# Expert stage of a two-block network: rows stationary instead of weights, weights split into high and rest, streamed in 8 KB pieces

## The chip, the core and the metric

The kernel runs on one NeuronCore of a Trainium2 chip. Its engines are TensorE (PE, with weight loads shown apart as PEld), VectorE (DVE), ScalarE (ACT), GpSimd (POOL) and SyncE (SP), which here mostly issues DMAs. Data lives in HBM (DRAM), in SBUF (128 partitions) and in PSUM, where TensorE writes. The metric is the device time of one execution in microseconds; less is better.

## What is computed

Two blocks of a network over 1024 tokens of 1024 features, in float32. The change touches the second half of the first block, a mixture of experts: each token picks a group, then two of its eight experts, and each expert is a gated two-layer product. Cut to that part:

```
g_sel = argmax(tok @ w_group + b_group)
top_l, top_i = top_k(e_logits[g_sel], 2)
weight = p_group * softmax(top_l)
expert = g_sel * 8 + top_i                    # 32 experts
# pairs (token, expert) sorted by expert into blocks of rows
xb = tok[rows_tok]
a = xb @ w_gate[e]                            # [rows,1024] @ [1024,512]
u = xb @ w_up[e]                              # [rows,1024] @ [1024,512]
y = (silu(a) * u) @ w_down[e]                 # [rows,512] @ [512,1024]
out = zeros.at[row_tok].add(y * weight)
```

## The kernel before

`build_program` runs `first_mixer`, `mixture` and `second_block` one after another. `mixture` has four stages, each a block of five engine programs that synchronise by semaphores: `norm_to_T` (normalises the rows, stores them in DRAM as `normed_rows`, turns them for the router and lets TensorE compute the logits), `route` (picks experts, gives each pair a row in a block), `experts`, and `combine`, which gathers each token's two result rows from the DRAM tensor `expert_rows`.

A block of `experts` holds up to CAP = 88 rows of one expert; there are 32 blocks, one for each expert, and a branch for overfull experts, which is not taken in these runs. For each block:

- POOL copies the block's 88 row numbers to `block_ids` (L1405) and gathers the rows from DRAM into one of three slots of `rows` by an indirect DMA (L1408).
- PE turns them with eight transposes into `x_ps` (`turn`, L1426), and DVE copies them to `xT` (`x_out`, L1512).
- PE computes gate and up, 64 matmuls each (L1436): a 128x128 piece of the weights is the stationary operand and 88 columns of `xT` stream. The operands are plain float32.
- ACT takes the silu (L1485), DVE multiplies by up into `hidT` (L1519).
- PE computes down, 16 matmuls (L1449): 88 columns of `hidT` stationary, 512 columns of `w_down` streaming.
- ACT and DVE copy the halves of `y_ps` into the single buffer `y_rows` (L1491, L1525), and SP stores them (L1378).

Weights come in three slots of 6 MB each (gate, up and down of an expert, 2 MB each), issued by SP (L1106) as soon as the matmuls that read a slot are done. Gate and up rows are 2 KB in DRAM, down rows 4 KB. The order on PE is gate and up of block b, turn of block b+1, down of block b. The engines' programs are `Fori` loops over blocks. The first two slots are loaded during `norm_to_T`, the third during `route`.

Elsewhere in the kernel large products are made of three float32r matmuls (`product`, L107): each operand is split into a high part, rounded to float32r by ACT (L147), and a rest, made by DVE (L151) as the difference; high by high, high by rest and rest by high are summed in PSUM.

Of the kernel before, what the change touches and what calls it, by code (L numbers as in the profile page):

```python
# [53 lines left out]
WSLOTS = 3  # L54
# [377 lines left out]
def norm_to_T(nc, m, name, hT, gamma=None, gamma_row=None, rows_out=None, x_ready=None, res_out=None,  # L432
# [13 lines left out]
    with ExitStack() as mem:  # L446
# [75 lines left out]
        def _(dve):  # L522
# [9 lines left out]
            for t in range(TT):  # L532
# [10 lines left out]
                else:  # L543
                    if t == 0:
                        dve.wait_ge(g_in, 16)
                    if t >= 2:
                        dve.wait_ge(turned, t - 1)
                        dve.wait_ge(stored[t % 2], 16 * (t // 2))
                    nc.vector.scalar_tensor_tensor(out=scaled[:, t % 2, :], in0=m.res[:, t, :],
                                                   scalar=rstd[:, t:t + 1], in1=g_row[:], op0=ALU.mult,  # L550
# [496 lines left out]
class Router:  # L1047


    def __init__(self, nc, m, mem):  # L1050
        def sb(name, shape, dt=F32):
            return mem.enter_context(nc.sbuf_tensor(name, shape, dt))

        self.w = sb("router_w", [P, KT, NL])
        self.b = sb("router_b", [P, NL])
        self.before = sb("before", [P, P])
        self.idx = sb("index_row", [P, 2, EXPERTS])
        self.limits = sb("limits", [P, FULL_BLOCKS - 1])
# [4 lines left out]
        self.ps = mem.enter_context(nc.psum_tensor("route_ps", [P, 2, BANK], F32))  # L1063

    def load(self, sp, A):
        sp.dma_start(self.w[:], A["w_router"].rearrange("(k p) n -> p k n", p=P)).then_inc(self.loaded, 16)
# [17 lines left out]
class ExpertWeights:  # L1084
# [3 lines left out]
    def __init__(self, m):  # L1088
        self.gate, self.up, self.down = [], [], []
        self.gate_in = [m.sem(f"w_gate_in{s}") for s in range(WSLOTS)]  # L1090
        self.up_in = [m.sem(f"w_up_in{s}") for s in range(WSLOTS)]
        self.down_in = [m.sem(f"w_down_in{s}") for s in range(WSLOTS)]

    def add_place(self, nc, mem):
        s = len(self.gate)
        self.gate.append(mem.enter_context(nc.sbuf_tensor(f"w_gate_sb{s}", [P, KT, D_EXPERT], F32)))
        self.up.append(mem.enter_context(nc.sbuf_tensor(f"w_up_sb{s}", [P, KT, D_EXPERT], F32)))
        self.down.append(mem.enter_context(nc.sbuf_tensor(f"w_down_sb{s}", [P, D_EXPERT // P, D], F32)))

    def load(self, engine, A, s, e, used=None):  # L1100

        for i, (w, name, arrived) in enumerate(((self.gate, "w_gate", self.gate_in), (self.up, "w_up", self.up_in),
                                                (self.down, "w_down", self.down_in))):
            if used is not None:
                engine.wait_ge(*used[i])
            engine.dma_start(w[s][:], A[name][0, bass.ds(e, 1)].rearrange("o (k p) n -> p (o k) n", p=P)) \  # L1106
                .then_inc(arrived[s], 16)


def route(nc, m, A, router, weights):  # L1110
# [3 lines left out]
    with ExitStack() as mem:  # L1114
# [50 lines left out]

        @block.sync
        def _(sp):

            weights.load(sp, A, WSLOTS - 1, WSLOTS - 1)
# [148 lines left out]
def experts(nc, m, A, weights):  # L1318


    with ExitStack() as mem:
# [4 lines left out]
        S = WSLOTS  # L1326
        FE = D_EXPERT // P
        idx = sb("block_ids", [CAP, S], I32)
        rows = sb("rows", [CAP, S, D])
        xT = sb("xT", [P, KT, CAP])  # L1330
        act_out = sb("gate_act", [P, FE, CAP])
        hidT = sb("hidT", [P, FE, CAP])
        y = sb("y_rows", [CAP, D])
        ps_x = mem.enter_context(nc.psum_tensor("x_ps", [P, KT, P], F32))
        ps_h = mem.enter_context(nc.psum_tensor("h_ps", [P, 2, FE, P], F32))
        ps_y = mem.enter_context(nc.psum_tensor("y_ps", [P, 2, BANK], F32))

        idx_set = [sem(f"block_ids_set{s}") for s in range(S)]
        rows_in = [sem(f"rows_in{s}") for s in range(S)]

        turned = sem("rows_turned")
        xT_done = sem("xT_done")
        gate_mm = sem("gate_mm")
        up_mm = sem("up_mm")
        act_done = sem("gate_act_done")
        hid_done = sem("hid_done")
        down_mm = sem("down_mm")
        y_left = sem("y_left")
        y_right = sem("y_right")
        y_out = sem("y_stored")  # L1350
        block = mem.enter_context(nc.Block())

        waited_sp = sem("waited_sp")
        waited_pool = sem("waited_pool")
        ROUNDS, REST = EXPERTS // S, EXPERTS % S
        LAST = EXPERTS - 1

        OVER_SLOT = REST
# [11 lines left out]
        def _(sp):  # L1370
            def reload(s, e, read):

                weights.load(sp, A, s, e, used=((gate_mm, read), (up_mm, read), (down_mm, read)))

            def store(b):
                sp.wait_ge(y_left, b + 1)
                sp.wait_ge(y_right, b + 1)
                sp.dma_start(m.y_dram[bass.ds(b * CAP, CAP), :], y[:]).then_inc(y_out, 16)  # L1378

            with sp.Fori(0, ROUNDS - 1) as i:  # L1380
                for s in range(S):
                    reload(s, i * S + (S + s), i * S + (s + 1))
                    store(i * S + s)
            for b in range(EXPERTS - S - REST, EXPERTS):
                if b + S < EXPERTS:
                    reload(b % S, b + S, b + 1)
                store(b)

            def over(j):
                e = sp.value_load(m.over_table[0:1, bass.ds(j, 1)], min_val=0, max_val=EXPERTS - 1)  # L1390
                reload(OVER_SLOT, e, j + EXPERTS)
                store(j + EXPERTS)

            count = over_blocks(sp, over)

            sp.wait_ge(y_out, (count + EXPERTS) * 16)
            sp.sem_inc(waited_sp, 1)

        @block.gpsimd
        def _(pool):  # L1400
            def gather(s, b, use, read=None):

                if read is not None:
                    pool.wait_ge(turned, read)
                nc.gpsimd.tensor_copy(idx[:, s:s + 1], m.row_ids[:, bass.ds(b, 1)]).then_inc(idx_set[s], 1)  # L1405
                pool.wait_ge(idx_set[s], use + 1)
                pool.sem_inc(waited_pool, 1)
                pool.indirect_dma_start(rows[:, s, :], None, m.hn_dram,  # L1408
                                        bass.IndirectOffsetOnAxis(ap=idx[:, s:s + 1], axis=0)).then_inc(rows_in[s], 16)

            for s in range(S):
                gather(s, s, 0)
            with pool.Fori(1, ROUNDS) as i:
                for s in range(S):
                    gather(s, i * S + s, i, read=(i - 1) * S + (s + 1))
            for s in range(REST):
                gather(s, ROUNDS * S + s, ROUNDS, read=(ROUNDS - 1) * S + s + 1)
            over_blocks(pool, lambda j: gather(OVER_SLOT, j + EXPERTS, j + ROUNDS, read=j + EXPERTS))

        @block.tensor  # L1420
        def _(pe):
            def turn(s, use):

                pe.wait_ge(rows_in[s], (use + 1) * 16)
                for k in range(KT):
                    last = nc.tensor.transpose(ps_x[:, k, 0:CAP], rows[:, s, k * P:(k + 1) * P], m.ident[0:CAP, 0:CAP])  # L1426
                last.then_inc(turned, 1)

            def gate_up(s, use, b):
                pe.wait_ge(xT_done, b + 1)  # L1430
                for i, (w, arrived, done) in enumerate(((weights.gate, weights.gate_in, gate_mm),
                                                        (weights.up, weights.up_in, up_mm))):
                    pe.wait_ge(arrived[s], (use + 1) * 16)
                    for f in range(FE):
                        for k in range(KT):
# [1176 lines left out]
```

## Time and profile before

| | us |
|---|---|
| median of 3 runs | 3107.51 |
| lowest and highest | 3106.19, 3111.67 |
| span of the profiled execution | 3109.3 |
| mean TensorE clock granted, share of full | 0.943 |

The profile is of one execution. No time of its own is given for it beside the span, from the first to the last instruction, which is 1.8 us above the median of the runs. Busy time of an engine is the time in which an instruction of it ran. Matmuls are pipelined: one that shows as 390 ns long may start 227 ns after the one before it, so the pace is read from starts, or from a count in a window.

### The profile page before, as it was taken

How to read it: one execution, taken by the hardware profiler on the slowest of the kernel's cores; microseconds unless marked ns; L12 is line 12 of the kernel's file. 1: busy time of each engine (PE TensorE's matmuls, PEld its weight loads, DVE VectorE, ACT ScalarE, POOL GpSimd, SP SyncE). 2: the span in 40 equal slices, each digit the busy share in tenths (PEclk: the TensorE clock that was granted, in tenths of full speed). 3: DMA queues.
4: the chain of work that ended last, by engine and by line, in shares of the span. 5: the costliest groups of instructions: out<-in, count | busy, mean ns of one | idle time of the engine just before them, and what ended most of it. 6: DMA issues, size and time to landing. Idle time of an engine off the chain costs nothing. (4 is left out here: it accounts for less than half of the span.)

```text
span 3109.3 us, 32228 instructions
## 1 busy us (share of the span) xinstructions
PE 2834.6 (91%) x13544; PEld 2152.5 (69%) x13544; DVE 948.2 (30%) x1118; ACT 597.1 (19%) x833; POOL 196.0 (6%) x176
## 2 busy tenths in 40 slices
PE   6799998785999999999299998999898999998998
PEld 2388553575878787878177776666576888886877
DVE  5423152423010101010621265111244344433343
ACT  1311111120000000000411254111223222222232
POOL 3210101000000000000420000000002000000000
PEclk9899999785899999999699999999898999999999
DMA  3151322026899999993521001111302111113323
GB/s 117 44 161 40 116 59 81 18 70 257 276 318 320 318 320 316 322 316 117 211 69 47 34 1 47 42 41 34 115 35 74 47 47 47 50 51 122 98 86 108
DMA packets 231333, 388.13 MB, mean 125 GB/s; under 512 B 11422, under 2 KB 110750, under 8 KB 231256
## 3 DMA queue, kind: packets, MB, share of 16 engines
q1 hardware_dynamic: 221768, 358.83, 34.6%
q0 software_dynamic: 9488, 28.22, 2.9%
q8 instruction: 55, 0.90, 0.1%
q14 instruction: 22, 0.18, 0.0%
HBM read 350.41 MB, written 39.74 MB: 125 GB/s over the span
## 5 line engine op out<-in xcount | busy, mean ns | idle before, releaser
L111 PE MATMUL up_ps<-hT_high,w_up_high 128*128 128x512 f32 x704 | 274.7, 390 | 7.3 <-PEq L446 7.3
L112 PE MATMUL up_ps<-hT_rest,w_up_high 128*128 128x512 f32 x704 | 274.6, 390 | 0.0
L113 PE MATMUL up_ps<-hT_high,w_up_rest 128*128 128x512 f32 x704 | 274.5, 390 | 0.0
L1436 PEld LDWEIGHTS h_ps<-xT,w_gate_sb 128*128 128x128 f32 x2048 | 240.1, 196 | 17.1 <-issue 15.9
L1436 PE MATMUL h_ps<-xT,w_up_sb 128*128 128x88 f32 x2048 | 240.5, 280 | 0.0
L1436 PE MATMUL h_ps<-xT,w_gate_sb 128*128 128x88 f32 x2048 | 239.5, 279 | 1.0 <-DVE xT L1512 1.0
L1436 PEld LDWEIGHTS h_ps<-xT,w_up_sb 128*128 128x128 f32 x2048 | 237.8, 196 | 0.0
L1449 PE MATMUL y_ps<-w_down_sb,hidT 128*88 128x512 f32 x512 | 228.7, 600 | 2.6 <-DVE hidT L1519 2.5
L1449 PEld LDWEIGHTS y_ps<-w_down_sb,hidT 128*88 128x88 f32 x512 | 78.4, 158 | 130.8 <-issue 126.5
L111 PE MATMUL down_ps<-w_down_high,prod_high 128*128 128x512 f32 x352 | 139.3, 396 | 20.6 <-DVE w_down_rest L151 12.9
L111 PEld LDWEIGHTS up_ps<-hT_high,w_up_high 128*128 128x128 f32 x704 | 132.6, 188 | 35.2 <-issue 7.7
L1519 DVE TENSOR_TENSOR hidT<-gate_act,h_ps 128x352 f32<-128x352 f32 x32 | 16.7, 521 | 445.6 <-PE h_ps L1436 445.6
L113 PEld LDWEIGHTS up_ps<-hT_high,w_up_rest 128*128 128x128 f32 x704 | 132.6, 188 | 27.8
L112 PEld LDWEIGHTS up_ps<-hT_rest,w_up_high 128*128 128x128 f32 x704 | 132.6, 188 | 27.5
L112 PE MATMUL down_ps<-w_down_rest,prod_high 128*128 128x512 f32 x352 | 138.4, 393 | 0.0
L113 PE MATMUL down_ps<-w_down_high,prod_rest 128*128 128x512 f32 x352 | 138.3, 393 | 0.0
L151 DVE TENSOR_TENSOR w_up_rest<-res,w_up_high 128x1024 fp32r<-128x1024 f32 x44 | 57.0, 1298 | 247.6 <-ACT w_up_high L147 247.6
L111 PE MATMUL gates_ps<-hT_high,gates_w_high 128*128 128x512 f32 x256 | 103.3, 404 | 7.5 <-DVE gates_w_rest L151 7.5
L1491 ACT ACTIVATE y_rows<-y_ps 88x512 f32<-88x512 f32 x32 | 19.0, 593 | 473.4 <-PE y_ps L1449 473.4
L111 PE MATMUL proj_ps<-hT_high,proj_w_high 128*128 128x512 f32 x256 | 100.7, 393 | 7.3 <-PEq L446 7.3
L147 ACT ACTIVATE w_up_high<-res 128x1024 fp32r<-128x1024 f32 x44 | 46.5, 1060 | 295.8 <-PE up_ps L113 295.8
L112 PE MATMUL proj_ps<-hT_rest,proj_w_high 128*128 128x512 f32 x256 | 100.5, 393 | 0.0
(311 smaller groups left out, 4498.7 us busy)
## 6 DMA issues: line engine op xcount, KB each, us to landing
w_gate_sb<-in_w_gate_dram SPq DMA_DIRECT2D x32, 2048.0 KB, 10.2
w_up_sb<-in_w_up_dram SPq DMA_DIRECT2D x32, 2048.0 KB, 11.5
w_down_sb<-in_w_down_dram SPq DMA_DIRECT2D x32, 2048.0 KB, 9.6
res<-in_w_in_dram SPq DMA_DIRECT2D x48, 512.0 KB, 4.0
res<-in_w_up_dram SPq DMA_DIRECT2D x44, 512.0 KB, 3.8
w_down_raw<-in_w_down_dram SPq DMA_DIRECT2D x44, 512.0 KB, 3.6
expert_rows<-y_rows SPq DMA_DIRECT2D x32, 352.0 KB
res<-in_x_dram SPq DMA_DIRECT2D x16, 512.0 KB, 7.2
```

The lines of the kernel that those rows point to most:

```text
L111: nc.tensor.matmul(out, w_high, x_high, start=start, stop=False)
L112: nc.tensor.matmul(out, w_high, x_rest, start=False, stop=False)
L113: return nc.tensor.matmul(out, w_rest, x_high, start=False, stop=stop)
L147: self.nc.scalar.activation(self.high_part[:, s], self.raw[s], ACT.Copy).then_inc(self.high_done[s], 1)
L151: self.nc.vector.tensor_tensor(self.rest_part[:, s], self.raw[s], self.high_part[:, s].bitcast(F32), ALU.subtract) \
L1436: last = nc.tensor.matmul(ps_h[:, i, f, 0:CAP], w[s][:, k, f * P:(f + 1) * P], xT[:, k, :], start=(k == 0), stop=(k == KT - 1))
L1449: last = nc.tensor.matmul(ps_y[0:CAP, half, :], hidT[:, f, :], weights.down[s][:, f, half * BANK:(half + 1) * BANK], start=(f == 0), stop= ...
L1491: nc.scalar.activation(y[:, 0:BANK], ps_y[0:CAP, 0, :], ACT.Copy).then_inc(y_left, 1)
L1519: nc.vector.tensor_tensor(hidT[:], act_out[:], ps_h[:, 1, :, 0:CAP], ALU.mult).then_inc(hid_done, 1)
```

## The change

In `experts` the gathered rows become the stationary operand of gate and up too, and all three products are made of float32r parts. Per block: the turned rows are split by ACT and DVE into `x_high` and `x_rest`; the gate and up weights stream, 512 columns at a time, into one PSUM bank each with 88 rows; silu and the multiplication work on rows; the hidden rows are turned back by four transposes (`turn_hidden`) and split into `hid_high` and `hid_rest`; down is made of parts as well. `in_products` and `out_products` issue 12 matmuls for a unit.

The weights come as units of 1 MB (8 KB on each of the 128 partitions, contiguous in DRAM): two each for gate, up and down. They pass through a ring of seven raw pieces and a ring of five split pieces (`ExpertWeights.high` on ACT, `ExpertWeights.rest` on DVE). `_units` fixes their order: the four gate and up units of expert e, then the two down units of expert e-1. Seven units are loaded during `norm_to_T`, none in `route`.

A partition now holds features 8p to 8p+7 instead of p, 128+p, ...; `norm_to_T` writes its rows in that order (through strided access patterns of one DVE instruction), and the router's weights are loaded to match. The loops are written out. Stores of `y_rows` (now two buffers) move from SP to POOL, and the copy of the row numbers goes away.

The core of the diff:

```diff
-WSLOTS = 3
+UNIT = 2 * D
+RAW_SLOTS = 7
+SPLIT_SLOTS = 5
...
+    def load(self, engine, n):
+        if n >= RAW_SLOTS:
+            engine.wait_ge(self.rest_done, n - RAW_SLOTS + 1)
+        e, i = UNITS[n]
+        engine.dma_start(self.raw[:, n % RAW_SLOTS, :], self.source(e, i)).then_inc(self.raw_in[n % RAW_SLOTS], 16)
+
+    def high(self, act, n):
+        act.wait_ge(self.raw_in[n % RAW_SLOTS], 16 * (n // RAW_SLOTS + 1))
+        if n >= SPLIT_SLOTS:
+            act.wait_ge(self.used, n - SPLIT_SLOTS + 1)
+        self.nc.scalar.activation(self.high_part[:, n % SPLIT_SLOTS, :], self.raw[:, n % RAW_SLOTS, :], ACT.Copy) \
+            .then_inc(self.high_done, 1)
+
+    def rest(self, dve, n):
+        dve.wait_ge(self.high_done, n + 1)
...
-                    for f in range(FE):
-                        for k in range(KT):
-                            last = nc.tensor.matmul(ps_h[:, i, f, 0:CAP], w[s][:, k, f * P:(f + 1) * P],
-                                                    xT[:, k, :], start=(k == 0), stop=(k == KT - 1))
...
+        def in_products(pe, out, s, i):
+
+            for kk in range(KT // 2):
+                k = (i % 2) * (KT // 2) + kk
+                last = product(nc, out[0:CAP, :], (x_high[:, k, :], x_rest[:, k, :]), weights.parts(s, kk * D_EXPERT),
+                               start=(k == 0), stop=(k == KT - 1))
+            return last
...
+            def gather(b):
+                if b >= S:
+                    pool.wait_ge(x_turned, b - S + 1)
+                pool.indirect_dma_start(rows[:, b % S, :], None, m.hn_dram,
+                                        bass.IndirectOffsetOnAxis(ap=m.row_ids[:, b:b + 1], axis=0)) \
+                    .then_inc(rows_in[b % S], 16)
+
+            def store(b):
+                pool.wait_ge(y_left, b + 1)
+                pool.wait_ge(y_right, b + 1)
+                pool.dma_start(m.y_dram[b * CAP:(b + 1) * CAP, :], y[:, b % S, :]).then_inc(y_out[b % S], 16)
+
+            gather(0)
+            gather(1)
+            for b in range(EXPERTS):
+                if b + S < EXPERTS:
+                    gather(b + S)
+                store(b)
...
+            turn(0)
+            for b in range(EXPERTS):
+                gate_up(b)
+                if b + 1 < EXPERTS:
+                    turn(b + 1)
+                if b:
+                    down(b - 1)
+                turn_hid(b)
+            down(EXPERTS - 1)
...
+            for b in range(EXPERTS + 1):
+                if b:
+                    hid_in(b - 1)
+                if b >= 2:
+                    y_half(b - 2)
+                if b < EXPERTS:
+                    for i in range(4):
+                        ahead(in_at(b, i))
+                    hidden(b)
+                    if b + 1 < EXPERTS:
+                        x_in(b + 1)
+                if b:
+                    ahead(out_at(b - 1, 0))
+                    ahead(out_at(b - 1, 1))
```

(S is 2 in the new `experts`; `ahead(n)` splits unit n+4; the last loop shown is DVE's.)

On POOL, in the middle of the expert stage, before the change: each gather stands behind a small copy and behind nothing else.

```order
L1405 COPY block_ids<-row_ids 88x1
L1408 DMA rows<-normed_rows,block_ids 88x1024
L1405 COPY block_ids<-row_ids 88x1
L1408 DMA rows<-normed_rows,block_ids 88x1024
L1413 UNCONDITIONAL_BRANCH
```

At the same place after the change (the store on L1497 was on SP before):

```order
L1490 DMA rows<-normed_rows,row_ids 88x1024 x3
L1497 DMA expert_rows<-y_rows 88x1024
L1490 DMA rows<-normed_rows,row_ids 88x1024
L1497 DMA expert_rows<-y_rows 88x1024
L1490 DMA rows<-normed_rows,row_ids 88x1024
L1497 DMA expert_rows<-y_rows 88x1024
```

The gather of block b+3 now comes behind the store of block b, so it waits for what the store waits for.

On DVE, one block of the loop before:

```order
L1519 TENSOR_TENSOR hidT<-gate_act,h_ps 128x352
L1508 REGISTER_ALU
L1512 COPY xT<-x_ps 128x704
L1524 REGISTER_ALU
L1525 COPY y_rows<-y_ps 88x512
```

And DVE's rows for one block after the change, from one split of the turned rows to the next:

```order
L1445 TENSOR_TENSOR x_rest<-x_ps,x_high 128x704
L1153 TENSOR_TENSOR expert_rest<-expert_raw,expert_high 128x2048 x2
L1452 TENSOR_TENSOR hid_rest<-hid_ps,hid_high 128x352
L1459 COPY y_rows<-y_ps 88x512
L1153 TENSOR_TENSOR expert_rest<-expert_raw,expert_high 128x2048 x4
L1437 TENSOR_TENSOR expert_hid<-gate_act,expert_up_ps 88x128x4
L1445 TENSOR_TENSOR x_rest<-x_ps,x_high 128x704
```

Three instructions a block have become ten, six of them over 2048 elements, and the copy of `y_rows` stands behind `hid_rest`.

## Rows read from the trace of the kernel before

**Rows 1.** The page: the span, and TensorE's busy time over it.

```profile
span 3109.3 us, 32228 instructions
PE 2834.6 (91%) x13544; PEld 2152.5 (69%) x13544; DVE 948.2 (30%) x1118; ACT 597.1 (19%) x833; POOL 196.0 (6%) x176
```

**Rows 2.** Busy time by stretch: columns in the first line; the expert stage.

```profile
core 0: us, PE busy (x) PEld busy (x) DVE busy (x) ACT busy (x) POOL busy (x), PEclk, DMA share, GB/s
763.00:785.00 22.00, 22.00 (x103) 22.00 (x104) 0.00 (x0) 0.46 (x1) 0.98 (x1) 0.50 0.37 121
...
791.00:1483.00 692.00, 689.38 (x4726) 544.54 (x4724) 65.21 (x94) 32.77 (x62) 32.53 (x56) 1.00 0.86 292
```

**Rows 3.** Timeline of one block: start us, us, engine, line.

```profile
1005.53 7.31 PE L1436 MATMUL h_ps<-xT,w_up_sb 128*128 128x88 f32 x64
...
1012.67 0.77 PE L1426 MATMUL x_ps<-ident,rows 88*128 88x88 f32 x8
...
1013.64 7.07 PE L1449 MATMUL y_ps<-w_down_sb,hidT 128*88 128x512 f32 x16 [0.19 <-DVE hidT L1519]
...
1020.55 7.27 PE L1436 MATMUL h_ps<-xT,w_gate_sb 128*128 128x88 f32 x64
...
1027.66 7.31 PE L1436 MATMUL h_ps<-xT,w_up_sb 128*128 128x88 f32 x64
```

**Rows 4.** Busy time by stretch: steady float32r products of 128x512 (feed-forward).

```profile
2400.00:2800.00 400.00, 400.00 (x1767) 331.20 (x1766) 163.29 (x130) 99.92 (x93) 0.00 (x0) 1.00 0.17 49
```

**Rows 5.** Groups of instructions (xcount | busy us, mean ns | idle before): work on DVE and ACT.

```profile
L151 DVE TENSOR_TENSOR w_down_rest<-w_down_raw,w_down_high 128x1024 fp32r<-128x1024 f32 x44 | 53.9, 1225 | 17.0 <-ACT w_down_high L147 17.0
L1292 DVE TENSOR_TENSOR at_row<-r_of,count_row 128x1408 f32<-128x1408 f32 x1 | 1.6, 1626 | 0.0
L1512 DVE COPY xT<-x_ps 128x704 f32<-128x704 f32 x32 | 28.5, 892 | 11.0 <-PE x_ps L1426 8.4
L1519 DVE TENSOR_TENSOR hidT<-gate_act,h_ps 128x352 f32<-128x352 f32 x32 | 16.7, 521 | 445.6 <-PE h_ps L1436 445.6
L1525 DVE COPY y_rows<-y_ps 88x512 f32<-88x512 f32 x32 | 22.0, 687 | 205.7 <-PE y_ps L1449 205.7
L147 ACT ACTIVATE w_down_high<-w_down_raw 128x1024 fp32r<-128x1024 f32 x44 | 46.0, 1044 | 6.0 <-DMA w_down_raw<-in_w_down_dram 6.0
L1491 ACT ACTIVATE y_rows<-y_ps 88x512 f32<-88x512 f32 x32 | 19.0, 593 | 473.4 <-PE y_ps L1449 473.4
```

**Rows 6.** Busy time by stretch: DMA with many loads queued, and in one block.

```profile
710.00:720.00 10.00, 10.00 (x49) 10.00 (x48) 0.00 (x0) 0.00 (x0) 0.00 (x0) 0.50 1.03 396
...
1005.53:1027.66 22.13, 21.94 (x155) 17.47 (x154) 2.10 (x3) 1.06 (x2) 1.16 (x2) 1.00 0.95 316
```

**Rows 7.** The gathers: issue (ns min/median/max) and landing, 1000 to 1400 us; the first one's timeline.

```profile
L1408 POOL DMA_INDIRECT rows<-normed_rows,block_ids x18: 980/984/987, 1014.7 to 1389.0; - x18
...
DMA to landing us min/median/max: 8.1/8.9/10.7
...
755.73 1.08 POOL L1408 DMA_INDIRECT rows<-normed_rows,block_ids  x1 [0.98 <-POOL block_ids L1405]
...
760.54 1.43 PE L1426 MATMUL x_ps<-ident,rows 88*128 88x88 f32 x8 [6.51 <-DMA rows<-normed_rows,block_ids]
```

**Rows 8.** Timeline of `combine`: gathers alone and beside DVE.

```profile
1494.37 0.94 POOL L1578 DMA_INDIRECT y_pairs<-expert_rows,pair_row  x1 [0.30 <-issue]
...
1498.10 2.60 DVE L1607 SCALAR_TENSOR_TENSOR res<-y_pairs,pair_w,res 128x1024 f32<-128x1024 f32 x2 [0.65 <-DMA y_pairs<-expert_rows,pair_row]
...
1498.56 1.63 POOL L1578 DMA_INDIRECT y_pairs<-expert_rows,pair_row  x1 [0.30 <-issue]
```

**Rows 9.** Stores issued by POOL (ns min/median/max), and the end of the stage.

```profile
L640 POOL DMA_DIRECT2D expert_rows<-res x23: 513/513/786, 156.5 to 167.9; - x23
...
1483.09 0.69 DVE L1525 COPY y_rows<-y_ps 88x512 f32<-88x512 f32 x1 [7.19 <-PE y_ps L1449]
...
1488.11 0.97 POOL L1578 DMA_INDIRECT y_pairs<-expert_rows,pair_row  x1 [98.11 <-SPq L1548]
```

**Rows 10.** Busy time by stretch: granted clock as float32r products of 512 columns begin.

```profile
2358.00:2362.00 4.00, 4.00 (x17) 3.24 (x17) 0.00 (x0) 0.00 (x0) 0.00 (x0) 0.94 0.54 148
```

More of the change, by code:

```diff
@@ L1100, in load, with __init__ @@
[L1100 to L1107, printed above, removed]
+    def __init__(self, nc, m, mem, A):
+        self.nc = nc
+        self.raw = mem.enter_context(nc.sbuf_tensor("expert_raw", [P, RAW_SLOTS, UNIT], F32))
+        self.raw_in = [m.sem(f"expert_raw_in{s}") for s in range(RAW_SLOTS)]
+        self.high_done = m.sem("expert_high_done")
+        self.rest_done = m.sem("expert_rest_done")
+        self.used = m.sem("expert_unit_used")
+        self.gate = A["w_gate"][0].rearrange("e (p k) n -> e p (k n)", p=P)
+        self.up = A["w_up"][0].rearrange("e (p k) n -> e p (k n)", p=P)
+        self.down = A["w_down"][0].rearrange("e (p f) n -> e p (f n)", p=P)
@@ new lines, in in_products, with out_products @@
+        def in_products(pe, out, s, i):
[4 more added lines that the diff above has]
+            return last
+        def out_products(pe, s, i):
+            for ff in range(FE // 2):
+                f = i * (FE // 2) + ff
+                for half in range(2):
+                    last = product(nc, ps_y[0:CAP, half, :], (hid_high[:, f, :], hid_rest[:, f, :]),
+                                   weights.parts(s, ff * D + half * BANK), start=(f == 0), stop=(f == FE - 1))
+            return last
@@ L1370, in _ @@
         def _(sp):
[L1371 to L1383, printed above, removed]
@@ L1396, in _ @@
-            sp.wait_ge(y_out, (count + EXPERTS) * 16)
-            sp.sem_inc(waited_sp, 1)
+                sp.wait_ge(weights.rest_done, j * 6 + N_UNITS)
+                for i in range(6):
+                    w = (weights.gate, weights.up, weights.down)[i // 2]
+                    sp.dma_start(weights.raw[:, i, :], w[bass.ds(e, 1), :, (i % 2) * UNIT:(i % 2 + 1) * UNIT]
+                                 .rearrange("o p n -> p (o n)")).then_inc(weights.raw_in[i], 16)
+            over_blocks(sp, over)
@@ L1420, in _ @@
+            count = over_blocks(pool, over)
+            pool.wait_ge(y_out[0], (count + EXPERTS // S) * 16)
+            pool.sem_inc(waited_pool, 1)
         @block.tensor
         def _(pe):
-            def turn(s, use):
-                pe.wait_ge(rows_in[s], (use + 1) * 16)
-                for k in range(KT):
[L1426 to L1433, printed above, removed]
-                    for f in range(FE):
-                        for k in range(KT):
-                            last = nc.tensor.matmul(ps_h[:, i, f, 0:CAP], w[s][:, k, f * P:(f + 1) * P],
-                                                    xT[:, k, :], start=(k == 0), stop=(k == KT - 1))
-                    last.then_inc(done, 1)
@@ new lines, in hid_in, with y_half, ahead @@
+            def hid_in(b):
+                dve.wait_ge(hid_high_done, b + 1)
+                hid_rest_part(dve)
+            def y_half(b):
+                dve.wait_ge(weights.used, out_at(b, 1) + 1)
+                if b >= S:
+                    dve.wait_ge(y_out[b % S], 16 * (b // S))
+                right(dve, b % S)
+            def ahead(n):
+                if n + SPLIT_SLOTS - 1 < len(UNITS):
+                    weights.rest(dve, n + SPLIT_SLOTS - 1)
+            x_in(0)
+            for n in range(SPLIT_SLOTS - 1):
+                weights.rest(dve, n)
```

370 lines of the change are left out of this document (228 added, 142 removed).

## The prediction

> **What bounds the kernel now.** I read the page first: TensorE is busy 91% of 3109.3 us [rows 1]. The change touches one stage, so next come the stretches of that stage. From 791 to 1483 us TensorE is busy 689.4 of 692 us at full clock, while DVE is busy 65 us and ACT 33 us; the first 22 us ran at half clock [rows 2]. Then the timeline of one block: one start of the up products to the next, 1005.53 to 1027.66, is 22.1 us, made of up (7.0 us to the turn), turn (1.0), down (6.9) and gate (7.1) with no gap over 0.5 us [rows 3]. So TensorE is the bound of this stage, and its neighbour is close: in the same block the DMA engines are busy 95% of the time [rows 6]. The stage lasts from the first gather at 755.7 to the first gather of `combine` at 1488.1, 732.4 us [rows 7, 9]. Everything below is a new time per block, P, and what is added once.
>
> **TensorE.** Removed: 128 matmuls of 88 columns and 16 of 512, 7.0 + 7.1 + 6.9 = 21.0 us. Added: 72 float32r matmuls of 512 columns. Their pace is 400 us / 1767 = 0.226 us [rows 4], where 128 columns are stationary; here it is 88, which can only make the weight load shorter. 72 x 0.226 = 16.3 us. The turn stays (0.8), four transposes come (half of it, 0.4). TensorE needs **17.5 us** a block, 4.5 less than now, if nobody keeps it waiting.
>
> **DVE and ACT.** Six rests of 2048 elements: 1024 take 1.225 and 1408 take 1.626 us [rows 5], a slope of 1.04 us per 1000, so 2048 take 2.29; doubling the first gives 2.45 as the upper bound. That is 13.7 to 14.7. The splits of the turned rows and of the hidden rows, the multiplication and the copy of y are 0.89, 0.52, 0.69, 0.69 (same sizes [rows 5]). The multiplication writes with a stride, which no row shows; between nothing extra and a doubling I take nothing, since it costs 0.7 at most. Sum **16.5 to 17.5 us**, plus ten handovers of some 0.06. ACT: six of 1.93 to 2.09 (from 1.044 [rows 5]) and four small ones under 0.8, about 14 us; it is not the bound. DVE went from 3 instructions to 10 and is now as full as TensorE.
>
> **DMA.** A block moves 6.29 MB of weights, and 0.36 MB each gathered and stored: 7.0 MB. With many loads queued the engines moved 396 GB/s; in the steady block only 316 at a share of 0.95, 333 if always busy [rows 6]. Bounds: 17.7 us and 21.0 us a block. I take a value near the first, 18.2, because seven units may be outstanding, which is the state of the fast row, where one or two loads were outstanding in the slow one; the pieces are also larger, whose effect no row shows. Against this stands a rule of the Trainium skill (DMA: Bandwidth & Descriptors, "Where 436 GB/s comes from"): what one core gets from HBM is about 358 GB/s. Here 396 GB/s were measured from HBM, so this trace does not agree; by the rule a block could not be under 7.0 / 358 = 19.6 us.
>
> **The circle through POOL.** This is the wait that the change adds, and I take it to decide. The gather of block b+3 stands behind the store of block b, which waits for y of block b; ACT and DVE copy that y only behind the split of hidden b+1, which waits for the turn of hidden b+1, the last thing TensorE does before gate and up of b+2. Then TensorE wants the rows of b+3 when gate and up are done. So from one arrival of rows to the next: turn 0.77 [rows 3], down 24 x 0.226 = 5.4 [rows 4], turn of hidden 0.45, hidden high about 0.5, hidden rest 0.52, y copy 0.69 [rows 5], store issue 0.51 [rows 9] and 0.3 between issues [rows 8], handovers 0.3: 9.4 us. Add what DVE is doing when hidden high is ready. After the arrival ACT splits the turned rows (turn and x high: 1.65 us), then highs one unit, so DVE starts its rests at 3.7 and ends the second at 8.3, while hidden high is ready at 7.2: 1.1 us more. Sum 10.5 us. Add the gather from issue to landing: 8.1 to 10.7 us, median 8.9, in the busy stage, 4.8 when the DMA engines were idle [rows 7]. With the median P = **19.4 us**; with 4.8 it is 15.3, and the circle is hidden behind the other bounds; with 10.7 it is 21.2. I take 8.8, close to the median, for two effects that pull apart: the store just ahead in the same queue lengthens the landing, and a P above the DMA bound of 18.2 leaves the load queue short, which shortens it. P = **19.3**.
>
> POOL's issue itself can be held up. A gather took 0.94 us alone and 1.63 beside a DVE instruction with both inputs in SBUF, which began 0.46 us before it and lasts 1.3: it ended with the rest of that instruction added [rows 8]. DVE's rests are such instructions, 2.29 long, and start right after the y copy. Bounds: 0 to 2.3 us a block, of which I put nothing into the sum since the second rest must first get its high part, and keep the end for the range. The Trainium skill states the same as a rule (SBUF — State Buffer, "Who interferes with whom"): a `tensor_tensor` with both inputs in SBUF contends with GpSimd's reads, and the later one blocks fully. By that rule P would be up to 21.6 us, and DVE would in turn wait behind POOL.
>
> **What is added once.** The gather can start at once, 1.2 us earlier than 755.7. Landing 4.8, turn 1.43 at half clock [rows 7], x high 0.8, one high 1.9, one rest 2.3: TensorE's first product is at 765.9. At half clock a unit is 5.4 instead of 2.7; the clock is up 4 to 8 us after such products begin [rows 10], where now it stayed at half over the first 30 us [rows 2]. I add 2.5. At the end: hidden split not covered 1.3, y copy and the wait for the store, now 5.0 from the copy's start at 1483.09 to 1488.11 [rows 9], on POOL some 0.9 more: 5.9. End of the stage = 765.9 + 2.5 + 32 P + 1.3 + 5.9 = **775.6 + 32 P**. It is 1488.1 now, so it breaks even at P = 22.3.
>
> The other edits I cost at nothing: fewer bytes fetched ahead (the seven units are there long before 760, and the third expert's load was on no path), the strided write in `norm_to_T` (ACT's squares and TensorE's logits cover it; uncovered, a microsecond for the first tile), the copy of row numbers (POOL waits anyway). Overfull experts do not occur. The programs are written out, so each engine fetches more instructions through the same DMA engines; no row of this stage prices it.
>
> **Sum.** P = 19.3 gives 775.6 + 617.6 = 1393.2, 94.9 us less than 1488.1. On the span of 3109.3 that is 3014.4; the median of the runs is 1.8 below the span, so **3013 us**.
>
> **Rivals.**
> - *No wait binds.* The gather lands in under 8 us, because the load queue is short when it is issued; TensorE, DVE and DMA all end between 17.5 and 18.5. P = 18.0: 775.6 + 576 = 1351.6, a gain of 136, 2971 us. For it: the circle is self-limiting. Against: three engines within 1 us of each other seldom overlap fully.
> - *DMA is the bound at its steady rate.* If stores and gathers between the loads, not a short queue, made the 333 GB/s, P = 21.0 at worst and 20.6 likely, with nothing else in the way: 775.6 + 659 = 1434.8, 3054 us. The page's 358 GB/s quoted above would be this rival with P = 19.6, 3022 us.
> - *Slower.* The circle with landing at 10.7 us and POOL held up by rests at 2.3 us: 10.5 + 10.7 + 2.3 = 23.5, 775.6 + 752 = 1527.6, a loss of 39.5, 3147 us. It decides from P = 22.3, which means landing plus hold-up of 11.8 us against 8.8 in my sum. For it: rows 8, and 8 KB pieces of load interleaved with the rows. Against: with P over 20 the load queue runs empty.
>
> **Chances.** Forecast (P 18.5 to 20.2) 0.42; no wait 0.22; DMA bound 0.16; a circle of 21 to 22.2, still a little faster or the same, 0.10; slower 0.10. The measurement can tell 0.2%, 6 us, from no change. Faster 0.86, same 0.04, slower 0.10. Range: the low end is P = 17.7 (DMA at 396 GB/s), a gain of 146: 2962. The high end is P = 21.5: 1463.6, a gain of 24: 3083. This leaves out about 0.15.
>
> **What would show it.** Right: blocks 19 to 20 us apart; before most turns TensorE waits 1 to 3 us for the DMA of `rows`; the wait is gone if the gather stands ahead of the store; DVE busy about 85%, DMA share near 0.9 with over 350 GB/s. DMA rival: TensorE's waits are on rests, DVE's on highs, ACT's on the raw pieces' DMA. Wrong altogether: float32r matmuls with 88 stationary columns slower than 0.23 us, rests over 2.5 us, a granted clock that drops in the waits, or gaps put down to issue.

## The result: 1.55% slower, and the profile after

The changed kernel takes 3156.7 us (median; 3155.1 to 3166.3) against 3108.7: a ratio of 1.0155, 95% interval 1.0143 to 1.0167. The forecast was 3013. The span of the profiled execution is 3164.5 us, 55 more than before [rows 1]. Rows of a profile are of one execution and can lie off the medians given: the one of the changed kernel is the slowest of its four, those of e8 (3143.0 us) and e12 (3069.3) are the fastest of theirs, and that of e2 (3157.9) ran slow after the expert stage, at a granted clock of 0.62 from 1600 to 2000 us against 0.98 in the stretch of the expert stage read below, so that e2's time is the median of its other four executions.

```profile
span 3164.5 us, 28100 instructions
...
PE 2753.3 (87%) x11368; PEld 2004.0 (63%) x11368; DVE 1414.1 (45%) x1342; ACT 994.7 (31%) x1089; POOL 244.5 (8%) x176
```

TensorE has less to do (2753 us busy, 2835 before) and the kernel is still longer. Where the time went is read from the gathers: start, duration, line. The first of the stage, two in its middle (the 5th and the 29th), and the first of `combine`:

```profile
755.14 1.09 POOL L1490 DMA_INDIRECT rows<-normed_rows,row_ids  x1 [211.11 <-issue]
...
1538.71 1.02 POOL L1757 DMA_INDIRECT y_pairs<-expert_rows,pair_row  x1 [10.21 <-SPq L1727]
```

The stage lasts 783.6 us instead of 732.4 [rows 7, 9], so 51 of the 55 us are in it. The 5th gather is issued at 831.06 and the 29th at 1404.68: 24 blocks in 573.6 us, **23.9 us a block**. The stretch from 850 to 1350 us:

```profile
core 0: us, PE busy (x) PEld busy (x) DVE busy (x) ACT busy (x) POOL busy (x), PEclk, DMA share, GB/s
850.00:1350.00 500.00, 411.20 (x1754) 274.69 (x1753) 345.48 (x210) 280.81 (x209) 59.10 (x42) 0.89 0.86 294
```

The longest waits from 850 to 1450 us (us in total, times, longest):

```profile
POOL expert_rows L1497 <- DVE y_rows L1459: 521.9, 25, 23.1
ACT x_high L1442 <- PE x_ps L1407: 157.3, 25, 7.7
PEld x_ps L1407 <- DMA rows<-normed_rows,row_ids: 118.3, 25, 5.9
PE x_ps L1407 <- DMA rows<-normed_rows,row_ids: 106.7, 25, 5.5
```

No engine is full: TensorE 82%, DVE 69%, ACT 56%, DMA 0.86 (before, TensorE was busy 689.4 of 692 us [rows 2]). In front of every turn TensorE waits some 4.3 us for the gathered rows, and the clock granted is 0.89 where it was 1.00. The gathers themselves, 1000 to 1400 us, take 2.2 us to issue and 11.4 to land (counted from the start of the issue), where it was 0.98 and 8.9 [rows 7]:

```profile
L1490 POOL DMA_INDIRECT rows<-normed_rows,row_ids x17: 2214/2227/2242, 997.9 to 1380.2; - x17
...
DMA to landing us min/median/max: 10.8/11.4/12.7
```

One turn of the circle through POOL, from the timeline (start, us, engine, line; in brackets the idle time before and what ended it):

```profile
1009.64 1.43 PE L1407 MATMUL x_ps<-ident,rows 88*128 88x88 f32 x8 [4.31 <-DMA rows<-normed_rows,row_ids]
...
1013.70 2.29 DVE L1153 TENSOR_TENSOR expert_rest<-expert_raw,expert_high 128x2048 fp32r<-128x2048 f32 x1 [0.91 <-ACT expert_high L1147]
1015.51 1.92 ACT L1147 ACTIVATE expert_high<-expert_raw 128x2048 fp32r<-128x2048 f32 x1 [1.85 <-PE y_ps L140]
1017.46 2.29 DVE L1153 TENSOR_TENSOR expert_rest<-expert_raw,expert_high 128x2048 fp32r<-128x2048 f32 x1 [1.48 <-ACT expert_high L1147]
1018.04 0.47 PE L1412 MATMUL hid_ps<-ident,expert_hid 88*128 88x88 f32 x4
...
1019.67 0.52 DVE L1452 TENSOR_TENSOR hid_rest<-hid_ps,hid_high 128x352 fp32r<-128x352 f32 x1
...
1020.11 0.68 DVE L1459 COPY y_rows<-y_ps 88x512 f32<-88x512 f32 x1
1021.32 4.49 DVE L1153 TENSOR_TENSOR expert_rest<-expert_raw,expert_high 128x2048 fp32r<-128x2048 f32 x2 [0.54 <-ACT expert_high L1147]
1021.35 0.59 POOL L1497 DMA_DIRECT2D expert_rows<-y_rows  x1 [21.18 <-DVE y_rows L1459]
...
1022.25 2.22 POOL L1490 DMA_INDIRECT rows<-normed_rows,row_ids  x1 [0.30 <-issue]
```

From the arrival of rows (1009.6) to the issue of the next gather (1022.25) are 12.6 us, and 11.4 later, at 1033.68, the next turn begins. Over the 20 rounds from 850 to 1350 us the means are 12.3 and 11.6, together 23.9, the pace that was measured. The clock over the same wait, the turn and the down products:

```profile
1005.40:1009.64 4.24, 0.00 (x1) 0.01 (x1) 2.42 (x2) 0.00 (x0) 0.00 (x0) 0.75 1.00 307
1009.64:1011.10 1.46, 1.46 (x9) 1.46 (x10) 0.00 (x0) 0.00 (x0) 0.00 (x0) 0.50 1.01 421
1011.10:1018.04 6.94, 6.94 (x25) 4.38 (x25) 3.76 (x3) 4.47 (x3) 0.00 (x0) 0.76 0.67 241
```

It falls to half while TensorE waits, the turn runs at half clock, and the stretch of the down products takes 6.9 us, where 24 at the full-clock pace of this trace (0.232 us each) would take 5.6. Not every turn is like this one: 12 of the 20 took 1.43 or 1.44 us, the others 0.8 to 1.1.

### The profile page after: what moved, and what is told of

It reads as the page before. It is cut to its first block and busy times, and to the rows that moved or that the text cites. A ratio compares the mean times of both kernels' runs of the same rounds, so it can differ in the third digit from the quotient of the medians.

```text
span 3164.5 us, 28100 instructions
## 1 busy us (share of the span) xinstructions
PE 2753.3 (87%) x11368; PEld 2004.0 (63%) x11368; DVE 1414.1 (45%) x1342; ACT 994.7 (31%) x1089; POOL 244.5 (8%) x176
## 5 line engine op out<-in xcount | busy, mean ns | idle before, releaser
L1153 DVE TENSOR_TENSOR expert_rest<-expert_raw,expert_high 128x2048 fp32r<-128x2048 f32 x192 | 436.8, 2291 | 112.1 <-ACT expert_high L1147 110.5
L1147 ACT ACTIVATE expert_high<-expert_raw 128x2048 fp32r<-128x2048 f32 x192 | 366.7, 1912 | 71.1 <-PE y_ps L140 53.2
L1407 PE MATMUL x_ps<-ident,rows 88*128 88x88 f32 x256 | 38.9, 320 | 132.0 <-DMA rows<-normed_rows,row_ids 132.0
L138 PE MATMUL y_ps<-expert_high,hid_high 128*88 128x512 f32 x256 | 123.5, 483 | 1.9 <-DVE y_rows L1459 1.9
L1407 PEld LDWEIGHTS x_ps<-ident,rows 88*128 88x128 f32 x256 | 31.7, 193 | 146.0 <-DMA rows<-normed_rows,row_ids 145.6
L139 PE MATMUL y_ps<-expert_rest,hid_high 128*88 128x512 f32 x256 | 119.7, 468 | 0.0
L140 PE MATMUL y_ps<-expert_high,hid_rest 128*88 128x512 f32 x256 | 117.5, 459 | 0.0
L138 PE MATMUL expert_gate_ps<-expert_high,x_high 128*88 128x512 f32 x256 | 103.5, 404 | 5.3 <-DVE expert_rest L1153 5.1
L139 PE MATMUL expert_gate_ps<-expert_rest,x_high 128*88 128x512 f32 x256 | 101.8, 398 | 0.0
```

The source lines that it names most:

```text
L138: nc.tensor.matmul(out, w_high, x_high, start=start, stop=False)
L139: nc.tensor.matmul(out, w_high, x_rest, start=False, stop=False)
L140: return nc.tensor.matmul(out, w_rest, x_high, start=False, stop=stop)
L1147: self.nc.scalar.activation(self.high_part[:, n % SPLIT_SLOTS, :], self.raw[:, n % RAW_SLOTS, :], ACT.Copy) \
L1153: self.nc.vector.tensor_tensor(self.rest_part[:, s, :], self.raw[:, n % RAW_SLOTS, :], self.high_part[:, s, :].bitcast(F32), ALU.subtract) ...
```

## The experiments

The theory: POOL's order closes a circle (rows arrive, down and turn of hidden, copy of y, store, gather, landing), and the circle sets the pace: each gather waits for work that waited for the gather before it. Rivals: the DMA engines are the bound at the rate they show (294 GB/s); or the order is harmless and the landing alone is long, for the size of the pieces or the store's bytes in the same queue. Below, the time of "a block" is taken from the 5th gather to the 29th, as above.

### e1: gathers ahead of stores

```diff
-            gather(0)
-            gather(1)
+            for b in range(S + 1):
+                gather(b)
             for b in range(EXPERTS):
-                if b + S < EXPERTS:
-                    gather(b + S)
+                if b + S + 1 < EXPERTS:
+                    gather(b + S + 1)
                 store(b)
```

> One edit to the changed kernel: POOL issues three gathers at the start and then the gather of block b+3 ahead of the store of block b, so a gather waits only for the turn that frees its slot. If the circle through POOL sets the pace (23.65 us a block in the profile after), TensorE's waits for rows go, blocks come 17.7 to 20 us apart, and the kernel gains 115 to 190 us: 2965 to 3040 us. If instead the DMA engines are the bound at the rate they had in the profile after (293 GB/s), the blocks stay 23 us or more apart, TensorE's waits move to the rests of the weights, and the time stays near 3157 us.

2995.1 us, ratio to the kernel before 0.9627 (0.9611 to 0.9643): 162 us less than the changed kernel, from the order of two instructions. 18.5 us a block. 850 to 1350 us, the gathers, and what ACT waits for:

```profile
850.00:1350.00 500.00, 484.51 (x2262) 326.38 (x2261) 437.76 (x271) 361.08 (x269) 102.18 (x52) 0.99 1.00 371
```

```profile
L1490 POOL DMA_INDIRECT rows<-normed_rows,row_ids x25: 975/2216/8200, 857.8 to 1301.8; - x25
...
DMA to landing us min/median/max: 11.4/12.6/17.4
```

```profile
ACT expert_high L1147 <- DMA expert_raw<-in_w_up_dram: 48.0, 46, 2.8
ACT expert_high L1147 <- DMA expert_raw<-in_w_down_dram: 33.0, 29, 3.0
```

The landing is longer than in the changed kernel (12.6 against 11.4), and TensorE no longer waits for it. The DMA engines are now busy all the time, ACT waits for raw pieces, and the rate is 371 GB/s: 294 was no bound but what the circle asked for. The rival on DMA falls for the changed kernel; once the circle is open it comes next, with TensorE (484.5 of 500 us busy) right beside it.

### e5 and e6: idle POOL is given work

```diff
                 pool.dma_start(m.y_dram[b * CAP:(b + 1) * CAP, :], y[:, b % S, :]).then_inc(y_out[b % S], 16)
+                for i in range(3):
+                    nc.gpsimd.memset(spare[:], 0.0).then_inc(spared, 1)
+                    pool.wait_ge(spared, 3 * b + i + 1)
```

> The changed kernel with three dependent fills of an unused tile on POOL between the store and the gather behind it, some 0.6 us each, 1.8 us a block. POOL is busy 11% of the stage, so by its load it could take them for nothing. If the circle through POOL's order sets the pace, they are added to every block: 29 or 30 blocks x 1.8 = 50 us, at most 58: 3200 to 3215 us. If the circle is not the cause, the time stays at 3157.

3262.5 us, 106 more, twice what was expected; 27.5 us a block, 3.6 more for fills that put off the gather by 1.7 (the store's start to the gather's start 2.6 us instead of 0.9). The rest is in the gather: issue 2.7, landing 13.1.

```profile
L1492 POOL DMA_INDIRECT rows<-normed_rows,row_ids x18: 2397/2722/2745, 858.7 to 1325.6; - x18
...
DMA to landing us min/median/max: 12.4/13.1/14.1
```

> The same three fills in the kernel that gathers ahead of the store. There the circle is open and the DMA engines were busy all the time (share 1.00 at 371 GB/s), so the fills should cost nothing: 2990 to 3000 us. If the pace of that kernel were still set through POOL, it would rise by 50 us as well.

2997.6 us (2995.4 to 3002.2), the same as e1. The same work in the same idle engine costs 106 us in one order and 2.5, less than the spread of the runs, in the other. That is the circle.

### e2 and e12: the store beside and in the queue

```diff
 (POOL)
                 pool.wait_ge(y_left, b + 1)
                 pool.wait_ge(y_right, b + 1)
-                pool.dma_start(m.y_dram[b * CAP:(b + 1) * CAP, :], y[:, b % S, :]).then_inc(y_out[b % S], 16)
 (ACT, y_half)
                 left(act, b % S)
+                act.wait_ge(y_left, b + 1)
+                act.wait_ge(y_right, b + 1)
+                act.dma_start(m.y_dram[b * CAP:(b + 1) * CAP, :], y[:, b % S, :]).then_inc(y_out[b % S], 16)
```

> The order of the changed kernel is kept (POOL still waits for both halves of y of block b before it gathers block b+3), but the store itself is issued by ACT, so it is neither in POOL's program nor in its DMA queue; ACT now waits for DVE's half of y, 1 to 2 us a block. If the wait in the order is the cause, little changes: 0.9 us of issue goes from the circle and perhaps 1 us of landing, 23.65 to some 22 us a block, a gain of 30 to 60 us, and TensorE still waits for rows. If the store's data ahead of the gather in the same queue is the cause, landing falls from 11.4 to 8 us or less and the gain is over 100 us.

3020.7 us, ratio 0.9724 (0.9702 to 0.9745): 136 us less, where I had expected 30 to 60 from the order alone, and over 100 only with a landing of 8 us or less. 19.5 us a block, issue 0.98, landing 8.5:

```profile
L1490 POOL DMA_INDIRECT rows<-normed_rows,row_ids x26: 976/976/979, 860.3 to 1348.7; - x26
...
DMA to landing us min/median/max: 7.2/8.5/11.6
```

TensorE still waits for rows (34.7 us from 850 to 1350, against 88.8 in the changed kernel), so the circle is still there, but it is near the pace of the DMA engines (share 0.97). The edit changes three things: the store leaves POOL's queue, its issue leaves the circle, and ACT's wait for DVE's half puts off the next high, so that no DVE rest runs when the gather is issued. e12 takes out the bytes alone (the rows that it does not write are filled with zeros early in the kernel, so its output is not that of the model):

```diff
-                pool.dma_start(m.y_dram[b * CAP:(b + 1) * CAP, :], y[:, b % S, :]).then_inc(y_out[b % S], 16)
+                pool.dma_start(m.y_dram[b * CAP:b * CAP + 1, :], y[0:1, b % S, :]).then_inc(y_out[b % S], 16)
```

> The changed kernel with its order, but each store from the expert stage writes one row of 4 KB instead of 88 (the other rows are filled with zeros during the first mixer's projection, 32 more stores of zeros there), so the output lacks most of what the experts add. The issue of the store, the order and the wait stay; only its 0.36 MB ahead of the gather in POOL's DMA queue is gone. If these bytes lengthen the landing, it falls from 11.4 to about 9.5 us and blocks come 2 to 4 us closer: 3040 to 3100 us. If the landing is long for the 8 KB pieces and DVE's hold alone, it stays at 11 and the time within 10 us of 3157.

3084.6 us (3069.3 to 3091.7), 72 less; issue 2.27, landing 9.6, clock 0.97, 20.8 us a block:

```profile
L1490 POOL DMA_INDIRECT rows<-normed_rows,row_ids x24: 2076/2268/2299, 863.7 to 1345.1; - x24
...
DMA to landing us min/median/max: 8.8/9.6/12.0
```

```profile
850.00:1350.00 500.00, 439.36 (x2011) 294.12 (x2010) 393.71 (x241) 321.66 (x241) 67.48 (x48) 0.97 0.91 319
```

So 1.8 us of the landing go with the 0.36 MB of the store ahead of the gather in the same queue. In this execution a block becomes shorter by 3.1: the wait shrinks, and with it the time at half clock (arrival to issue is 10.9 us in the mean, 12.3 in the changed kernel). By the medians it is 72 us over 32 blocks, 2.3 each.

### e3: small rows, and e4: the clock

```diff
-        self.gate = A["w_gate"][0].rearrange("e (p k) n -> e p (k n)", p=P)
+        self.gate = A["w_gate"][0].rearrange("e (k p) n -> e p k n", p=P)
```

(up and down alike, and the loads' access patterns to match; the experts then multiply features with other rows of the weights)

> Only the source of the weight loads changes: the units of 1 MB are read as rows of 2 KB (gate, up) and 4 KB (down), as the kernel before did, while the gathered rows keep their new order of features; so the experts multiply features with other rows of the weights, the amount of work and of bytes being the same. If pieces of 8 KB between the gathered rows lengthen the landing, it falls from 11.4 towards the 8.9 us of the kernel before, blocks come 21 to 22 us apart and 50 to 80 us are gained. If piece size does not matter, landing stays at 11 and the time within 10 us of 3157.

3118.2 us (3111.7 to 3128.9), 38 less, short of the 50 to 80 that were expected; 22.7 us a block. Landing (850 to 1350 us):

```profile
DMA to landing us min/median/max: 9.7/10.3/11.1
```

The pieces of 8 KB account for 1.1 us of the 11.4, not for the whole 2.5 over the kernel before.

```diff
             def turn(b):
+                if b:
+                    for _ in range(16):
+                        nc.tensor.matmul(ps_idle[0:CAP, :], x_high[:, 0, :],
+                                         x_high[:].rearrange("p k c -> p (k c)")[:, 0:BANK], start=True, stop=True)
                 pe.wait_ge(rows_in[b % S], 16 * (b // S + 1))
```

> Added: 16 float32r matmuls of 512 columns (some 3.7 us, results unused) in front of each turn, where TensorE waits 4.3 us for rows. The circle stays. If the fall of the clock in that wait is part of the price, the turn takes 0.8 instead of 1.4 us and the down products 5.6 instead of 6.9, blocks come 21.7 us apart and the gain is about 60 us. If the clock does not matter, since the circle is set by DMA, ACT, DVE and POOL, the time stays at 3157 or rises a little.

3139.0 us (3132.6 to 3142.2), 18 less instead of 60. The clock stayed up, 850 to 1350 us:

```profile
850.00:1350.00 500.00, 474.35 (x2192) 318.03 (x2191) 362.23 (x220) 296.25 (x220) 61.89 (x44) 0.99 0.89 307
```

A block took 22.9 us. The part from arrival to issue was 10.7 in the mean (10.4 in most rounds), against 12.3 with the falling clock and 10.5 in my sum; from issue to the next turn it was 12.2 against 11.6, with the landing grown from 11.4 to 12.1. So 1.6 us a block were won and 0.6 lost again; why the landing grew I can't say.

### e7: rests in halves

```diff
-        self.nc.vector.tensor_tensor(self.rest_part[:, s, :], self.raw[:, n % RAW_SLOTS, :],
-                                     self.high_part[:, s, :].bitcast(F32), ALU.subtract).then_inc(self.rest_done, 1)
+        for i in range(2):
+            c = slice(i * UNIT // 2, (i + 1) * UNIT // 2)
+            last = self.nc.vector.tensor_tensor(self.rest_part[:, s, c], self.raw[:, n % RAW_SLOTS, c],
+                                                self.high_part[:, s, c].bitcast(F32), ALU.subtract)
+        last.then_inc(self.rest_done, 1)
```

> The changed kernel with each rest of 2048 elements made by two DVE instructions of 1024. In the profile after each gather's issue took 2.22 us instead of 0.98 and ended with the DVE rest that was running. If the hold-up lasts until the running DVE instruction ends, issue takes at most 1.23 + 0.9, and since the first half began some 0.9 us before, it falls to about 1.3: some 0.9 us a block or 25 to 30 us less, from which later ends of the rests (0.16 us each) may take up to 10: 3125 to 3150 us. If the hold-up is no lock but slow handling under load, issue stays at 2.2 us and the time does not fall.

3144.3 us (3135.3 to 3147.8), 12 less, and the issue of the gather fell from 2.22 to 1.08 us:

```profile
L1493 POOL DMA_INDIRECT rows<-normed_rows,row_ids x22: 1014/1082/1127, 853.0 to 1345.0; - x22
...
DMA to landing us min/median/max: 9.5/10.7/11.5
```

The hold-up ends with the DVE instruction in progress, as expected. A block takes 23.5 us, 0.4 less: of the 1.1 us gained in the issue 0.7 arrived in the landing, and the two halves cost DVE 0.07 more a unit.

### e8: y before hidden

On ACT and on DVE `y_half(b - 2)` moves ahead of `hid_in(b - 1)`.

> The changed kernel with the copies of y of block b ahead of the split of hidden b+1 on ACT and on DVE, instead of behind it. y is ready 0.5 us before the hidden is turned; what comes out of the circle is the turn of hidden (0.5), its high (0.5) and its rest (0.5), but DVE is in a rest until 1.0 us later than that, and TensorE gets its hidden part later only where it has slack. Circle theory: 1 to 2 us a block come out, the fall of the clock with them, 30 to 60 us less, 3095 to 3125 us. If another wait sets the pace, nothing changes.

3157.5 us (3143.0 to 3164.1): no gain in the median, against 30 to 60 expected. The timeline shows why:

```profile
1013.31 2.29 DVE L1153 TENSOR_TENSOR expert_rest<-expert_raw,expert_high 128x2048 fp32r<-128x2048 f32 x1 [1.34 <-ACT expert_high L1147]
...
1015.52 0.68 DVE L1459 COPY y_rows<-y_ps 88x512 f32<-88x512 f32 x1
1016.12 0.51 DVE L1452 TENSOR_TENSOR hid_rest<-hid_ps,hid_high 128x352 fp32r<-128x352 f32 x1
1016.77 0.59 POOL L1497 DMA_DIRECT2D expert_rows<-y_rows  x1 [20.32 <-DVE y_rows L1459]
```

In either order DVE is in a rest until then, so the turn of hidden and its high were not on the path; only the 0.5 us of the hidden rest could leave it. The store is issued 0.57 us after the copy ends, as in the changed kernel (0.56), and the gather's landing was 12.1 us instead of 11.4 in the profiled run. There the part from arrival to issue did fall (11.4 us in the mean, 12.3 before the edit), and half of that went into the landing; the spread of the four executions, 21 us, is wider than what is left. My account of which steps lie in the circle was too simple here, though the circle itself was not at stake.

### e9 to e11: what bounds it once the circle is open

> Both edits together: gathers ahead, and stores issued by ACT. With the circle open the store's queue should not matter any more: DMA moves the same bytes at 371 to 377 GB/s, so the time should be that of gathers first alone, 2985 to 3005 us. If the stores in POOL's queue cost DMA time of their own, it falls by over 10 us; if ACT's wait for DVE's half of y matters, it rises.

2995.3 us, ratio 0.9632 (0.9616 to 0.9649): the same as e1, as expected. Landing is 9.4 us here, 12.6 there; it does not matter. But the DMA engines, though busy all the time, hold up nobody here: no engine waits for raw pieces, and what ACT waits for is that TensorE frees a split piece (850 to 1350 us):

```profile
ACT expert_high L1147 <- PE expert_gate_ps L140: 137.4, 27, 5.4
```

TensorE is busy 97.5% of the time at full clock, 18.0 us of a block by my sum at 0.232 us a product, and waits some 0.5 us a block for DVE (the multiplication and the rest of the turned rows): 18.5, the pace. So once the circle is open TensorE and DMA are bounds of nearly the same height. In e1 it is the raw pieces that come last, as shown above.

> Gathers first, with the weights read as rows of 2 KB (gate, up) and 4 KB (down), so the experts multiply features with other rows of the weights; the amount of work is the same. Now the DMA engines are the bound, so the size of pieces shows in the rate: if 8 KB pieces give a better rate than 2 and 4 KB, the stage moves under 370 GB/s and the time rises by 10 to 40 us over 2995; if only the number of loads outstanding made the rate (333 GB/s per full share before, 371 with seven outstanding), the time stays within 6 us of 2995.

3017.2 us, 22 more than e1, from which it differs in the rows alone. 850 to 1300 us in this kernel, in e1, and in e9:

```profile
850.00:1300.00 450.00, 424.27 (x1959) 283.01 (x1958) 373.26 (x232) 308.20 (x231) 97.14 (x46) 0.98 1.04 361
```

```profile
850.00:1300.00 450.00, 437.40 (x2053) 295.24 (x2052) 395.59 (x246) 326.25 (x244) 99.47 (x48) 0.99 1.02 377
```

```profile
850.00:1300.00 450.00, 438.96 (x2045) 291.27 (x2044) 390.92 (x245) 316.71 (x245) 23.44 (x24) 1.00 1.00 380
```

The DMA engines move 361 GB/s in rows of 2 and 4 KB, and 377 to 380 in pieces of 8 KB. Divided by the share, as the 333 of the kernel before was [rows 6], that is 347, and 370 to 380. So the size of the pieces gives 23 GB/s (e10 to e1), more than the 14 between the kernel before and e10. That those 14 come with the loads outstanding is not shown: in e9 a load lands 8.1 us after its issue (median) and one is issued every 3.1 us, so two or three of 1 MB are outstanding, and the rate is the highest of all.

```diff
-RAW_SLOTS = 7
-SPLIT_SLOTS = 5
+RAW_SLOTS = 9
+SPLIT_SLOTS = 4
```

> Gathers first, with nine raw pieces and four split ones instead of seven and five (the same space). Two more units of 1.05 MB are fetched before the stage, when the DMA engines are idle; if the DMA is the bound of the stage at 377 GB/s, 2.1 MB less are 5.6 us: 2988 to 2992 us. If the splits, only three units ahead of TensorE instead of four, become the bound, the time rises above 3000.

2988.8 us (2988.6 to 2991.8), ratio 0.9617 (0.9601 to 0.9634), the best version, on top of e1's order: 6 us less than e1 for 2.1 MB less in the stage, as a DMA bound says. TensorE is busy 99.9% from 850 to 1050 us, while the pieces fetched ahead last, and 96% from 1050 to 1250.

## Why the prediction was wrong

**The step that failed** is the sum of the circle through POOL. I named it as the wait that decides, and gave 10.5 us from arrival to issue and 8.8 to land, 19.3 in all. Measured, from arrival to issue and from issue to the next turn: 12.3 and 11.6, 23.9 in the mean. Of the 4.6 us that are missing in my sum 2.8 lie in the landing and 1.8 before it. The mechanism held (e1, e5, e6); both parts were taken too short:

| term | mine | measured | shown by |
|---|---|---|---|
| store's bytes ahead in the queue, in the landing | offset against a short load queue | 1.8 | e12 |
| POOL held up by a DVE rest, in the landing | 0 (bound 2.3) | 1.2 of issue, 0.7 in the landing | e7 |
| pieces of 8 KB, in the landing | 0, no row | 1.1 | e3 |
| turn at half clock | 0.77 | 1.43 in 12 of 20 turns | timeline after |
| second rest ends after the arrival | 8.3 | 10.1 in the turn shown | timeline after |

The single effects on the landing overlap and don't add up exactly (1.8 + 0.7 + 1.1 on top of the 8.9 of before would be 12.5; 11.4 was measured). The last two rows of the table are one cause that is missing in my sum: a wait of 4.3 us lowers the clock, the turn and the first down unit run at half clock, the second high waits for that unit, DVE's second rest for the high, and the copy of y for the rest. The wait makes itself longer. e4 shows its size: with the clock up, the part from arrival to issue is 10.7, close to the 10.5 that I had worked out for a full clock. I had put a falling clock only among the things that would make the prediction wrong, not into the price of the circle.

**The reasoning behind the wrong choice**: I set two unknowns of the landing against each other and called the median of before "close". But the row came from a queue with no store ahead of the gather and with DVE mostly idle, and these differences to the new place pointed to longer. The one that points the other way, a DMA queue that runs shorter, is there (share 0.86) and did not win. And the hold-up was put at zero, for the second rest had first to get its high part, with the end kept for the range. [rows 8] had shown a gather held up, and the timeline after has the next rest begin at 1021.32, 0.9 us ahead of the gather.

**What held.** The formula 775.6 + 32 P gives 1540.4 for P = 23.9; the stage ended at 1538.7. TensorE's pace: 0.232 us a product of 512 columns from the timeline (forecast 0.226). Rests took 2.29 us, as worked out, and highs 1.91. The multiplication with the strided write took 1.01 instead of 0.69.

**What met the number by luck.** The rival "slower", P = 23.5 and 3147 us, has the right mechanism and comes within 10 us of 3156.7, and its chance of 0.10 and a range that ended at P = 21.5 were too low. But its terms are not those measured: it has 13.0 for landing and hold-up, where landing, hold-up included, was 11.4, and 10.5 from arrival to issue, where it was 12.3; it knows nothing of the clock, and the two errors cancel. Nor does e1 bear the forecast out, though its 2995 us lie only 18 below it: the forecast had the circle as the bound, and in e1 the circle is open. What e1 does bear out is the DMA term, 18.2 us a block in the sum against a pace of 18.5, with TensorE's 18.0 just below.

**The two rules.** The Trainium skill's rule on the shared port (SBUF — State Buffer, "Who interferes with whom") is borne out for POOL: issue of a gather 2.22 us beside rests of 2.29, 1.08 beside rests of half the length (e7), 0.98 where no rest runs (e2). That DVE waits behind POOL in turn, the other half of what I took from it, is not seen: the two rests from 1021.32 took 4.49 us together, beside the gather's issue. The Trainium skill's figure of about 358 GB/s from HBM for one core (DMA: Bandwidth & Descriptors, "Where 436 GB/s comes from") is not what these runs show: 377 to 380 GB/s over 450 us in e1, e9 and e11, some 5% of it stores.

## What to carry to other kernels

When an instruction is moved to another engine's queue, write down what now stands behind it there, and follow that back to the instruction itself: if it comes round, the sum of the whole round is a bound on the pace, whatever the load of the engines, and giving an idle engine a little work (e5, with e6 beside it) tells at once whether there is such a round. Price its steps as they will be in the new place: at half clock where the engine waits first (4.3 us here), and behind the bytes that share the queue. Then look whether the order alone can open it: here the next block's input was queued behind the last block's output, and changing that made the same edit 3.7% faster than the kernel before instead of 1.55% slower.

## What the runs showed of the hardware that I had not expected

- A gather's landing was 12.6 us with no harm (e1), and 11.4 with much (the changed kernel): the number to watch is who waits, not the latency.
- 1.7 us put into the circle cost 3.6 us a block (e5): issue (2.7 us) and landing (13.1) grew with it.
- With the circle open the issue of a gather took up to 8.2 us (e1), beside DVE rests that follow one another. The plain store is not held up so: in the timeline above it is issued 0.03 us after a rest began and took 0.59 us, the gather behind it 2.22.
- DMA rate divided by the share: 347 GB/s in rows of 2 and 4 KB (e10), 370 to 380 in pieces of 8 KB (e1, e11, e9), 333 in the kernel before. With 380 in e9 only two or three loads of 1 MB were outstanding.
